# Other order of the router's products, shared buffers for its tables, and two ring places filled earlier, in a one-core decoder layer

## What is computed

```python
h = layer_norm(x, ln0_g, ln0_b)
mix = token_mixer(h, mem, w_in, ..., w_br, w_o)
h = layer_norm(alpha * h + mix, ln1_g, ln1_b)
logits = h @ w_router + b_router
top_logits, top_idx = lax.top_k(logits, 4)
w = softmax(top_logits)
# per expert e, for the tokens that chose it:
gate, up = split(xb @ w_gate_up[e] + b_gate_up[e])
y = (clip(up) + 1) * (min(gate, 7) * sigmoid(1.702 * gate)) @ w_down[e] + b_down[e]
out = layer_norm(alpha * h + sum(weight * y), ln2_g, ln2_b)
```

## Time and profile before

| | us |
|---|---|
| median of 3 runs | 1257.62 |
| lowest, highest | 1257.22, 1257.68 |
| the profiled execution: its own time | 1255.7 |
| its span | 1254.0 |
| mean granted TensorE clock | 0.994 of full |

### The profile page before, as it was taken

How to read it: one execution, slowest core, us unless ns; L and a number is a source line. 1 busy time by engine, 2 the same in 40 slices (tenths; PEclk the granted TensorE clock), 3 DMA queues, 4 the chain that set the end, 5 groups by cost and what they waited for, 6 DMA issues and landing times.

```text
span 1254.0 us, 17233 instructions
## 1 busy us (share of the span) xinstructions
PE 1213.0 (97%) x7155; PEld 613.1 (49%) x7155; DVE 390.5 (31%) x768; ACT 243.5 (19%) x402; POOL 148.7 (12%) x106
## 2 busy tenths in 40 slices
PE   8999999999999999999999999999999999999995
PEld 8999999998733333333333333333333333333332
DVE  6675633335522222222222222222222222222224
ACT  5764354544210000000000000000010000000001
POOL 7454323555100000000000000000000000000000
PEclk9999999999999999999999999999999999999999
DMA  9644231875899999999999999999999999999994
GB/s 335 221 148 143 70 136 67 330 292 201 353 409 429 428 429 428 427 429 429 429 428 429 429 429 428 429 428 430 428 429 427 427 427 428 429 427 428 428 427 198
DMA packets 53388, 453.45 MB, mean 362 GB/s; under 512 B 6925, under 2 KB 7002, under 8 KB 28762
## 3 DMA queue, kind: packets, MB, share of 16 engines
q1 hardware_dynamic: 53338, 452.71, 87.0%
HBM read 451.64 MB, written 1.05 MB: 361 GB/s over the span
## 4 chain that ended last, share of the span: by engine, by line
PE 78%; DMA 8%; SPq 5%; DVE 3%; ACT 3%; issue 2%; POOL 0%; DVEq 0%; ACTq 0%
PE bank L1419 29%; PE bank L1491 15%; DMA late<-in_w_gate_up_dram 8%; PE bank L1209 6%; SPq L807 5%; PE bank L1210 5%; PE bank L1211 5%; PE bank L1504 4%; PE bank L1390 4%; PE bank L1405 2%; PE bank L1479 1%; ACT late L1181 1%; ACT w_hi L1069 1%; PE bank L1499 1%; DMA raw<-in_w_mem_kv_dram 0%
## 5 line engine op out<-in xcount | busy, mean ns | idle before, releaser
L1419 PE MATMUL bank<-late 128*64 128x512 f32 x1536 | 343.5, 595 | 5.4 <-DMA late<-in_w_gate_up_dram 5.4
L1491 PE MATMUL bank<-late 128*64 128x512 f32 x1024 | 229.6, 601 | 6.0 <-ACT late L1181 6.0
L1419 PEld LDWEIGHTS bank<-late 128*64 128x64 f32 x1536 | 106.7, 137 | 223.2 <-issue 209.6
L1491 PEld LDWEIGHTS bank<-late 128*64 128x64 f32 x1024 | 71.3, 138 | 142.4 <-issue 128.6
L1209 PE MATMUL bank<-act_hi,w_hi 128*128 128x256 f32 x448 | 129.5, 289 | 1.9 <-DVE early L1699 1.4
L1210 PE MATMUL bank<-act_lo,w_hi 128*128 128x256 f32 x448 | 125.8, 281 | 0.0
L1211 PE MATMUL bank<-act_hi,w_lo 128*128 128x256 f32 x448 | 125.7, 281 | 0.0
L1834 DVE TENSOR_SCALAR late<-bank 128x512 f32<-128x512 f32 x32 | 22.1, 692 | 308.9 <-PE bank L1419 308.9
L1419 PE MATMUL bank<-raw,late 128*64 128x512 f32 x512 | 116.7, 598 | 1.5 <-DMA raw<-in_w_gate_up_dram 1.5
L770 POOL TENSOR_TENSOR w_lo<-raw,w_hi 128x1024 fp32r<-128x1024 f32 x33 | 81.9, 2483 | 102.1 <-ACT w_hi L1069 102.0
L1209 PEld LDWEIGHTS bank<-act_hi,w_hi 128*128 128x128 f32 x448 | 84.3, 188 | 4.1 <-DVE early L1699 2.0
(11 more groups left out here) (321 smaller groups left out, 1186.4 us busy)
## 6 DMA issues: line engine op xcount, KB each, us to landing
late<-in_w_gate_up_dram SPq DMA_DIRECT2D x96, 2048.0 KB, 37.1
late<-in_w_down_dram SPq DMA_DIRECT2D x64, 2048.0 KB, 36.5
raw<-in_w_gate_up_dram SPq DMA_DIRECT2D x32, 2048.0 KB, 35.2
raw<-in_w_in_dram SPq DMA_DIRECT2D x8, 2048.0 KB, 9.0
early<-in_w_in_dram SPq DMA_DIRECT2D x6, 2048.0 KB, 8.1
raw<-in_w_br_dram SPq DMA_DIRECT2D x3, 2048.0 KB, 7.6
raw<-in_w_mem_kv_dram SPq DMA_DIRECT2D x8, 512.0 KB, 11.2
raw<-in_w_o_dram SPq DMA_DIRECT2D x1, 2048.0 KB, 8.5
```

What stands on the lines that cost most here:

```text
L1419: ins = mm(bk[64 * c:64 * c + 64, :], x_slotT[:, k % 4, 64 * (k // 4):64 * (k // 4) + 64], w[:, kk, at + 512 * c:at + 512 * (c + 1)], star ...
L1491: ins = mm(ps[3][64 * c:64 * c + 64, :], hidT[:, kk, 64 * q:64 * q + 64], w[:, kk, c * 512:(c + 1) * 512], start=(q == 0 and kk == 0), sto ...
```

## The change

- PE: the first half of `logits(0)` now stands between the turning of tile 0 and the turning of tile 1, in place of ten `keep_warm` products. The second half follows the turning of tile 1, then `logits(1)`. The rank products are interleaved with `residual(0, *)`; the expert counts go to bank 3 behind them with a semaphore of their own (`counted`). `residual(1,0)` moves from ahead of the gather to behind it, in place of four `keep_warm` products; `residual(1,1)` moves into the first expert, behind its first chunk. Eight `keep_warm` products between the turned tokens and `bias` are gone, and `bias` no longer waits for the tokens but for its row (`row_made`).
- DVE: the first one-hot table is built directly behind the ranks; the weights (reciprocal and two products) and the counts come after it. The first tokens are scaled in two halves (`first_tokens`), and PE waits for each half apart.
- ACT: two of the four copies of `x1T(0,0)` stand ahead of the square root of tile 1's norm.
- POOL: `alpha_ident` is made at the end of the mixer and not near its start.
- SP: the router's weights are loaded late in the mixer and not near its start. Ring places 6 and 8 are filled behind chunk 0, when all branch sums are done; 7, 9 and 11 when the last `wo` product is done, with no further wait.
- Memory: the router's tables, `wr`, and the turned tokens lie in scratch and buffers that are dead then, and no longer in ring places.

```diff
+        BEHIND_BRANCHES = (EC, EC + 2)
@@ SP, the first fill
             for c in range(RAW):
                 raw_spent(sp, N_MIX - RAW + (c - N_MIX) % RAW)
                 chunk_dma(sp, c, w_gate_up[0, 0], w_down[0, 0], *ring_place(c)[0:2])
+                if c == 0:
+                    wait_sums(sp, KD)
+                    for m in BEHIND_BRANCHES:
+                        chunk_dma(sp, m - EC, w_gate_up[0, 1], w_down[0, 1], *ring_place(m)[0:2])
             sp.wait_ge(bank_full[bank_of(("wo", 1, 1))], turn_of(("wo", 1, 1)))
             for m in range(EC, RING):
-                if m == SPARE:
-                    continue
-                if m == SPARE - 1:
-                    sp.wait_ge(x1_added, 2 * NT)
-                if m == RING - 1:
-                    sp.wait_ge(onehots, 1)
-                chunk_dma(sp, m - EC, w_gate_up[0, 1], w_down[0, 1], *ring_place(m)[0:2])
+                if m != SPARE and m not in BEHIND_BRANCHES:
+                    chunk_dma(sp, m - EC, w_gate_up[0, 1], w_down[0, 1], *ring_place(m)[0:2])
@@ PE
+            def logit_rows(t, ks):
+                u = ("logits", t)
+                bk = ps[bank_of(u)]
+                if ks.start == 0:
+                    pe.wait_ge(bank_free[bank_of(u)], turn_of(u) - 1)
+                    pe.wait_ge(router_in, 32)
+                for k in ks:
+                    if k % 4 == 0:
+                        h = ("x1T", t, k // 4)
+                        pe.wait_ge(bank_free[bank_of(h)], turn_of(h))
+                    ins = mm(bk[:, 0:NE], x1T[t][:, k, :], wr[:, k, :], start=(k == 0), stop=(k == KD - 1))
...
                 elif kind == "x1T":
                     t, j = s[1:]
                     if s == ("x1T", 1, 0):
-                        keep_warm(10, ps[7])
+                        logit_rows(0, range(4))
                     pe.wait_ge(ln_done, NT + t + 1)
...
+                if first:
+                    pe.wait_ge(row_made, 1)
+                    pe.wait_ge(ebias_in, 128)
+                else:
+                    pe.wait_ge(tokens_in, i + 1)
                 bias()
...
+                    if q == 0 and first:
+                        residual(1, 1)
...
-            residual(1, 0)
-            residual(1, 1)
             pe.wait_ge(bank_free[bank_of(("rank", 0))], turn_of(("rank", 0)))
             pe.wait_ge(onehots, 1)
             gather()
-            keep_warm(4, ps[3])
+            residual(1, 0)
             turn_tokens(0)
-            keep_warm(8, ps[3])
-            pe.wait_ge(ebias_in, 128)
             gate_up(0, item_places(0), first=True)
```

More of the change, by code:

```diff
@@ L1048, in silu, with turned_half @@
                 a.activation(qkvT[:, n, :], qkvT[:, n, :], ACT.Silu).then_inc(silu_done, 1)
+            def turned_half(t, ks):
+                u = ("x1T", t, 0)
+                act.wait_ge(bank_full[bank_of(u)], turn_of(u))
+                for k in ks:
+                    ins = a.activation(x1T[t][:, k, :], ps[bank_of(u)][:, k * P:(k + 1) * P], ACT.Identity,
+                                       scale=small_cols[:, ROW_G + k:ROW_G + k + 1],
+                                       bias=small_cols[:, ROW_B + k:ROW_B + k + 1])
+                return ins
             act.wait_ge(consts, 2)
@@ L1079, in _ @@
                 elif kind == "ln" and s[1] == 1:
+                    if s[2] == 1:
+                        turned_half(0, range(2))
                     ln_root_of(*s[1:])
@@ L1152, in _ @@
                     a.copy(act_hi[:, s[1], :], bank(("br", 0, s[1]))).then_inc(sum_hi, 1)
[L1153 to L1161, removed]
+                elif kind == "x1T" and s[2] == 0:
+                    t = s[1]
+                    ins = turned_half(t, range(2, 4) if t == 0 else range(4))
+                    ins.then_inc(free, 1)
                 elif kind == "logits" and s[1] == 1:
@@ L1300, in _ @@
                 bk = ps[b]
-                if kind not in ("vm", "wo") and unit_at[s] >= BANKS:
+                if kind not in ("vm", "wo", "logits") and unit_at[s] >= BANKS:
                     pe.wait_ge(bank_free[b], turn_of(s) - 1)
@@ L1785, in _ @@
                     top_four(t)
[L1786 to L1793 removed]
                 elif kind == "rank":
                     full()
+                    v.wait_ge(r_mask, 2)
                     for t in range(NT):
[L1798 to L1800 removed]
+                        ins = d.scalar_tensor_tensor(out=ranks[:, t, 0:NE], in0=mask[:, t, :], scalar=-NOT_HERE,
+                                                     in1=bk[:, t * NE:(t + 1) * NE], op0=ALU.mult, op1=ALU.add)
+                    ins.then_inc(free, 1)
                     v.wait_ge(free, turn_of(s))
```

100 lines of the change are left out of this document (57 added, 43 removed).

## The result

| | before | changed |
|---|---|---|
| median of 20 runs each, us | 1255.84 | 1259.89 |
| lowest, highest | 1254.09, 1257.86 | 1256.79, 1262.33 |
| ratio, 95% interval | | 1.0031 [1.0024, 1.0038] |
| profiled execution: own time, span | 1255.7, 1254.0 | 1259.89, 1258.1 |
| its mean granted clock | 0.994 | 0.989 |

The changed kernel is slower by 3.9 us (3.0 to 4.8). I had forecast 1260.6: 1255.7 for the profiled execution of before, 1.9 for the median above it, and 2.95 for the change. The kernel before came out 1.8 us lower beside the change than in the three runs shown ahead, so the base of the sum was 1.8 too high and the difference of 2.95 was 1.0 too low. The two errors have opposite signs: that the absolute figure is off by only 0.7 is luck.

The account below looks back on a forecast made before the run. The weights' stream was taken to set the end, following PE's release of chunk 4. `gate_up` 1.95 us later, with `residual(1,1)` 2.95, gave 1255.7 + 2.95 = 1258.65, by the median 1.9 above it 1260.6; range 1256.5 to 1263.0.

Parts of the forecast that it names:

- What sets the end: Weights' stream: the end follows PE's release of chunk 4, which lets chunk 16 be issued, and moves by as much.
- The idle stretch and the fall: Router on PE: 3.3 us without work until bank 0 is released at 326.3; clock falls to half between 325 and 328.5.
- Half clock on narrow products: Router's logits on PE: each record takes 0.229 us at half clock instead of 0.117.
- Back before the gather: End of the router on PE: clock returns to full at 336 to 337, so the gather starts at 339.85.
- rival 3: Clock stays low through the residuals and into the gather: +3.9 to +5.5, and 1.0, 1262.5 to 1264.1 us; chance 0.17.
- case 1: Half clock through the router, back before the gather: `gate_up` 1.95 us later, chunk 4 freed 2.95 later, 1260.6 us; chance 0.33.
- At full clock: Router to first expert: -1.0 at the gather, -1.65 from there to `gate_up`, +1.0 for `residual(1,1)`, in sum -1.65 us.
- The order's term: Router on PE at full clock: tile 1's turning behind half of `logits(0)`; DVE takes the logits, and masks finish, 1.4 us late.
- The early chunks at 0: Ring: two chunks sent at about 301 fill it 10 us earlier but gain nothing by themselves, priced at 0.
- rival 5: Ring's backlog was the bound, not chunk 4; decides only if PE starts over 2.5 us earlier; 1255.0 us, chance 0.05.
- The residual in the expert: `residual(1,1)` inside the first expert, ahead of chunk 1: 1.0 us lost for every chunk behind it, chunk 4 included.

Follow-up runs that it names:

- warm: The changed kernel with the ten `keep_warm` products put back ahead of the first half of `logits(0)`; median 1254.16 us, ratio to the kernel before 0.9999.
- before_no_warm: The kernel before without its ten `keep_warm` products between the turnings of tile 0 and tile 1; median 1258.78 us, ratio 1.0021.
- order: The changed kernel with all eight logits products of tile 0 behind both turnings, as before, still without the ten `keep_warm`; median 1257.47 us, ratio 1.0020.
- no_early: The changed kernel with ring places 6 and 8 filled with the others, not behind the branch sums; median 1260.98 us of five runs, ratio 1.0045.
- both: The changed kernel with the old order of turning and logits and the ten `keep_warm` products back; median 1254.75 us, ratio to the kernel before 0.9988.
- moved_residuals: As both, but `residual(1,0)` behind the expert counts and `residual(1,1)` behind the gather, none in the first expert; median 1251.51 us, ratio 0.9960.
- moved_in_expert: As moved_residuals, but `residual(1,1)` in the first expert again and four `keep_warm` products in its place behind the gather; median 1255.08 us, ratio 0.9998.
- moved_split: As moved_residuals, but the first half of `logits(0)` ahead of tile 1's turning, `keep_warm` kept; median 1254.07 us, ratio 0.9988.
- bank3: The changed kernel with `logits(0)` in free bank 3, so its first half doesn't wait for bank 0, no `keep_warm`; median 1258.53 us, ratio 1.0014.
- both_no_early: As both, but ring places 6 and 8 filled late, without the early chunks; median 1255.48 us, ratio to the kernel before 0.9993.
- moved_no_early: As moved_residuals, but ring places 6 and 8 filled late, without the early chunks; median 1255.51 us, ratio to the kernel before 0.9999.
- moved_warm_expert: As moved_residuals, plus seven `keep_warm` products in the idle stretch ahead of the first expert's `down`; median 1251.30 us, ratio 0.9971.

## Why the prediction came out right, and where its steps did not

**What sets the end: right.** Span less chunk 16's issue stayed within 0.9 us in the eight kernels named above.

**The idle stretch and the fall: right.** 3.3 us forecast, 3.36 measured; half clock from about 326.5 (said 326.6). warm and before_no_warm show it from both sides, by the medians: the products back in the changed kernel, -5.7 us; taken out of the one before, +3.1. The order of the products isn't what loses the clock: order, with the old one, lost it too.

**Half clock on narrow products: right in kind, a little too dear.** Said 0.229 a record, measured 5.17/24 = 0.215. That brought DVE to the logits at 331.67 (said 332.2) and the masks to 337.1 (338.0). By the rule of the Trainium skill (TensorE: Matmul & The Clock Gate, section LDWEIGHTS), P/1.2 ns for a load of P columns, by estimate 107 ns for 128, with no term for the clock, the records would have kept their 0.117; here the trace disagrees, 0.215 at 1.2 GHz.

**"Back before the gather" is the step that failed.** The likeliest case had the clock back at 336 to 337. In the changed kernel's profiled execution, whose time is also the median, it came back at 343.5: both residuals 2.06 instead of one, the gather 3.41 instead of 1.9. `gate_up` began at 346.58 where 344.45 was forecast. That is rival 3, to which I gave 0.17. Its row was there: nothing dense lay between 323 us and the gather. It doesn't fail always: no_early, the same program on PE, had case 1 nearly to the letter (back near 337.5, gather 339.20 where 339.85 was forecast, `gate_up` 343.75 where 344.45 was), and eight of the changed kernel's twenty runs have a mean clock of 0.991 or 0.992, near the 0.992 of that execution, at 1256.8 to 1258.7 us. What decides between the two courses stays open.

**A term that I left in unseen made up for it.** The distance from `gate_up` to chunk 16 was 24.14 before and 24.05 now, with the 1.0 us of `residual(1,1)` in it. The execution of before had a half-clock stretch of its own in the first expert (the turning's 1.02 us), the changed one did not (0.64 at 365.96). I carried the one of before into the sum. 2.1 us too little at `gate_up`, 1.1 too much behind it: chunk 16 was forecast at 369.6 and came at 370.63, the span 1.1 longer than the sum. That these two nearly met is luck, and with the base 1.8 too high it is why the figure looks better than the working was.

**At full clock: about right.** The sum was -1.65. warm, which is the changed kernel with the clock mostly held, has -1.7 by medians but only -0.1 by its ratio (0.9999, that is -1.9 to +1.5), since four of its twelve runs have a mean clock of 0.991. At equal clock it has 1253.2, 1253.5 and 1254.8 at 0.996, 0.995 and 0.994, against 1254.2, 1255.5 and 1255.7: -0.8 to -2.0; at 0.991, 1258.6 against 1257.1, +1.5. The order's term in it, masks 1.4 us later, was measured as 1.16: masks done 11.84 us behind the first turning in warm, 10.68 before. That both, with the old order, isn't faster than warm by the medians (1254.75, 1254.16) doesn't speak against that; those two are too scattered to settle it.

**The early chunks at 0: right here, and rival 5 had the condition.** It was to decide when PE's start is earlier by over 2.5 us. moved_residuals has `gate_up` 3.6 us earlier than before, and there they are worth 4.0 us.

**The residual in the expert: sized too small.** Its products take 1.16 us (350.17 in the changed kernel), but moved_in_expert lost 3.6 by medians and 3.6, 3.9 and 4.1 at the three clocks that it shares with moved_residuals, one run each of the latter. Of the 3.5 us between the two profiled spans, 1.44 came from a fall of the clock in the mixer (below), 0.88 from the release of chunk 4 (`gate_up` to chunk 16 25.38 against 24.50; at full clock it is 1.25, above), and 1.2 lies behind chunk 16 (887.5 against 886.3). For the last I have only an argument. DMA has an empty queue when chunk 12 goes out; with the residual chunks 13 and 14 follow at 4.7 and 9.8 us, as long as they take to land, so none is ever queued, and without it at 3.4 and 8.6. The windows agree: 372 against 398 GB/s over 50 us is 3.0 us of transfer less, 1.4 of it from chunk 12's later start. moved_split, which has no residual there, is a control: 348 GB/s in the same 50 us, 5.8 us less, of which 5.65 is chunk 12's later start, so only 0.2 is left where moved_in_expert has 1.6. Rival 5 had spoken of the backlog; a queue run dry was nobody's. What part of the 3.6 us each of these has over many runs stays open.

## What to carry to other kernels

Before you take filler products off PE or put narrow ones in their place, read the granted clock of the stretch behind them: a forecast saving at full clock of 1.65 us became a loss of 3.9 because 3.4 us of waiting stood where 2.4 of filler had been. A wait bought in that way is paid for by everything that follows until the clock comes back, here 7 to 17 us later, the gather too. And work that is moved for its own length should be put where its engine waits, not ahead of the release that sets the end: with order and filler alike, the residuals in the idle stretches made the kernel 3.2 us faster by the medians than both, and moved_in_expert lost 3.6 of it again.

## What the runs showed that I had not expected

Half clock can last 17 us. With turnings, logits, residuals and rank products alone PE stayed at 1.2 GHz from 326.5 to 343.5 (changed; 326.3 to 343.3 in bank3), although it was busy in nearly every us of it. With the same products it lasted 10 us in no_early.

One and the same idle stretch sometimes loses the clock and sometimes not. In the mixer, untouched by any edit here, PE waits 2.16 us at 295 to 297. The execution of before held its clock through it; that of both did not, in stretches of 1 us of PE:

```profile
296.00:297.00 1.00, 0.00 (x0) 1.00 1.07 459
297.00:298.00 1.00, 0.63 (x5) 1.00 0.80 344
298.00:299.00 1.00, 1.00 (x7) 0.52 0.01 0
299.00:300.00 1.00, 1.00 (x5) 0.50 0.00 0
```

Everything behind it came 1.5 us later (first turning at 323.41 instead of 321.90). The same 1.4 to 1.8 us stands in the profiles of before_no_warm, both_no_early, moved_split, moved_in_expert and moved_no_early. So a single profile of this kernel says nothing on 1.5 us, and a row 1.5 us late is first to be looked for upstream. The wait of 1.88 us in the first expert behaves alike: the next turning took 0.64 us in warm, order and the changed kernel, 1.02 to 1.06 before, in both and in bank3.

Idle stretches that came before a fall were 3.36, 2.16, 2.00, 1.88 and 1.65 us, the last with one us of narrow products behind it; 1.08 held in warm. In both, both_no_early and moved_no_early the clock fell behind logits at full clock that had only 0.20 or 0.21 us idle ahead of them; in moved_residuals, moved_in_expert and moved_warm_expert, with the same products up to there, it held. The length of the idle stretch doesn't separate the cases, and what does stays open.
